# A rebuilt S5 front: injections ahead of one response round, each bank of sums opened once, and 3 of 32 modulation pieces behind the mixer

## The reference, cut to what matters

```python
mod = silu(c) @ w_mod + b_mod                    # 9 rows x 16384 numbers in all
h = modulate(rmsnorm(x, g), sh1, sc1)
lam_bar = exp(lam * dt); b_bar = ((lam_bar - 1) / lam) * b_mat
bu = einsum("blgp,gnp->blgn", u, b_bar)          # 64 groups g of 16 channels p, 64 complex states n
h = associative_scan(h[t] = lam_bar * h[t-1] + bu[t])
y = real(einsum("blgn,gpn->blgp", h, c_mat)) + d_skip * u
a, g = split(gelu(y) @ w_glu); out = a * sigmoid(g)
x = x + ga1 * out
x = x + ga2 * peer(modulate(rmsnorm(x, g2), sh2, sc2))   # gathers 128 expert rows for every row
```

## Time and profile before

| | us |
|---|---|
| timed, median of 3 runs | 3435.63 |
| timed, lowest to highest | 3426.26 to 3446.24 |
| profiled execution: span | 3430.0 |
| busy PE / DVE / ACT / POOL | 2541.4 / 2329.2 / 1302.1 / 1277.8 |
| DMA moved | 1284.73 MB, mean 375 GB/s |

### The profile page before, as it was taken

How to read it: one execution, slowest core, us unless ns; L and a number is a source line. 1 busy time by engine, 2 the same in 40 slices (tenths; PEclk the granted TensorE clock), 3 DMA queues, 4 the chain that set the end, 5 groups by cost and what they waited for, 6 DMA issues and landing times.

```text
span 3430.0 us, 62993 instructions
## 1 busy us (share of the span) xinstructions
PE 2541.4 (74%) x25173; PEld 935.2 (27%) x25173; DVE 2329.2 (68%) x5485; ACT 1302.1 (38%) x4056; POOL 1277.8 (37%) x1133
## 2 busy tenths in 40 slices
PE   4878997868668766668878887878587677666665
PEld 3756322323003200112235452224132032001000
DVE  8753885897866776465553458776888867764655
ACT  3441333333333333344433225553443343333333
POOL 0010343444444444433411227563444444443442
PEclk8979998878667766778999898888787787667667
DMA  9966999999999999999955369999999999999997
GB/s 325 348 241 267 398 413 414 415 403 411 426 426 414 413 426 424 410 420 399 395 180 235 118 227 371 355 411 412 394 421 410 426 421 414 423 425 385 424 426 318
DMA packets 178977, 1284.73 MB, mean 375 GB/s; under 512 B 22264, under 2 KB 23264, under 8 KB 30744
## 3 DMA queue, kind: packets, MB, share of 16 engines
q0 software_dynamic: 151696, 1109.99, 79.0%
q1 hardware_dynamic: 26416, 170.18, 13.1%
q10 hardware_dynamic: 576, 0.59, 0.0%
HBM read 1268.49 MB, written 12.18 MB: 373 GB/s over the span
## 4 chain that ended last, share of the span: by engine, by line
PE 36%; DMA 34%; DVE 19%; ACT 6%; issue 3%; POOL 1%; SPq 0%; another core or an unknown queue 0%; DVEq 0%; ACTq 0%; PEldq 0%; POOLq 0%
DMA arena<-peer_uv,arena 31%; PE psum L2948 13%; DVE arena L2315 9%; PE psum L2875 6%; PE psum L2834 3%; PE psum L3355 2%; DMA arena<-b_mod 2%; PE psum L3106 1%; PE psum L3037 1%; DVE arena L2225 1%; ACT arena L1604 1%; ACT arena L1601 1%; DVE arena L2329 1%; PE psum L2702 1%; DVE arena L1891 1%
## 5 line engine op out<-in xcount | busy, mean ns | idle before, releaser
L2948 PE MATMUL psum<-arena 32*32 32x512 f32 x16384 | 1470.3, 791 | 720.7 <-ACT arena L1604 652.3
L1267 POOL DMA_INDIRECT arena<-peer_uv,arena x1040 | 1160.5, 1116 | 1703.0 <-PE psum L2948 1482.7
L2315 DVE SCALAR_TENSOR_TENSOR arena<-arena 128x1024 f32<-128x1024 f32 x1040 | 1273.5, 1228 | 687.8 <-DMA arena<-peer_uv,arena 670.3
L1591 ACT ACTIVATE arena<-arena 128x1 f32<-128x1 f32 x944 | 190.9, 202 | 1390.8 <-DVE arena L2315 1383.4
L2948 PEld LDWEIGHTS psum<-arena 32*32 32x32 f32 x16384 | 215.8, 117 | 1799.3 <-ACT arena L1604 1584.5
L1604 ACT ACTIVATE arena<-arena 128x32 f32<-128x32 f32 x928 | 298.2, 321 | 30.3
L1601 ACT ACTIVATE arena<-arena 128x1 f32<-128x1 f32 x944 | 277.8, 294 | 30.7
L2875 PEld LDWEIGHTS psum<-arena 128*128 128x128 f32 x2048 | 241.5, 195 | 68.6 <-issue 66.9
L2875 PE MATMUL psum<-arena 128*128 128x128 f32 x2048 | 258.8, 282 | 1.1 <-ACT arena L1528 1.1
L2834 PE MATMUL psum<-arena 128*128 128x512 f32 x256 | 126.0, 625 | 3.2 <-ACT arena L1488 2.4
L2702 PE MATMUL psum<-arena 128*9 128x128 f32 x2048 | 78.8, 317 | 58.4 <-DMA arena<-b_mod 58.3
(11 more groups left out here) (352 smaller groups left out, 2430.8 us busy)
## 6 DMA issues: line engine op xcount, KB each, us to landing
arena<-w_mod SPq DMA_DIRECT2D x64, 1024.0 KB
arena<-peer_wq SPq DMA_DIRECT2D x16, 2048.0 KB, 11.4
arena<-peer_uv,arena POOLq DMA_INDIRECT x1040
arena<-w_glu SPq DMA_DIRECT2D x5, 2048.0 KB, 7.3
arena<-mod_rows SPq DMA_DIRECT2D x5, 1024.0 KB
arena<-w_o SPq DMA_DIRECT2D x1, 4096.0 KB
arena<-x_after_layer SPq DMA_DIRECT2D x7, 512.0 KB
arena<-mod_rows SPq DMA_DIRECT2D x6, 512.0 KB
```

What stands on the lines that cost most here:

```text
L1267: pool.indirect_dma_start(ring[r], None, a[f"peer_uv{t // 5}"], bass.IndirectOffsetOnAxis(ap=ix, axis=0)).then_inc(landed[r], 16)
L1591: act.activation(col, col, ACT.Gelu_apprx_tanh).then_inc(s_gl, 1)
L2315: dve.scalar_tensor_tensor(out=u, in0=u, scalar=GELU_IN if beside_exps(t, m) else 1.0, in1=h, op0=ALU.mult, op1=ALU.mult, accum_out=at(DOT ...
L2948: ins = pe.matmul(acc_of(t, i, c), diag[rows, r, :], ring[r][rows, D + 512 * c:D + 512 * (c + 1)], start=(m == 0), stop=last, skip_group_c ...
```

## The change

The modulation pieces are loaded up to four ahead (`DEEP`), each at places of its own from a written list; where a place is still in use within those four, the load waits for the products that read it. Pieces 29 and 30 are multiplied after the last "y" round and piece 31 after the first `w_glu` products, so 29 pieces instead of 32 stand ahead of the first "y" round. The loads of the first small parameters come first, the prompt rows behind pieces 0 to 3, and the four reads of modulation rows that the norm needs go from SP's queue to ACT's.

The "u" turns are eight rounds of 8 groups. The "i" rounds no longer alternate with "k" rounds; there is one "k" round for all 64 groups, in four column groups, behind the last "i". Its matmuls open each bank once (`start=(slot == 0)`), and 16 small matmuls with the diagonal `d_eye` add the skip term d, so the skip product and its sum on DVE go. The kernel is placed behind a zero pad of 112 columns, so that the "t" matmuls write full width and one ACT copy of 128x2048 replaces four. The copies of "i" rounds 0, 1 and 3 are made by ACT, those of round 2 by DVE. The states are placed in four segments, the first two by ACT as the scan gets there, the last two by DVE. The gelu reads the "y" sums from PSUM. Loops that a counter ran are written out.

```diff
+MOD_TURNS = (29, 30)
+MOD_NORM = 31
+DEEP = 4
...
+        MOD_PLACES = [(MT[0], MT[1]), (MT[2], MT[3]), (MC[0], MC[1]), (MH[0], MH[1]), (MT[0], MT[1]), (MT[2], MT[3]),
...
+                      (MT[0], MT[1]), (MT[2], MT[3]), (MH[0], MH[1]), (MX[0], MX[1]), (MX[2], MX[0]), (MH[0], MH[1]),
+                      (MX[1], MX[2]), (MX[0], MX[1]), (MH[0], MH[1]), (MX[2], MX[0]), (MX[1], MX[2]), (MR[0], MR[1]),
+                      (MJ[0], MJ[1]), (MW[0], MW[1])]
...
-        ROUNDS = ([("m", 0), ("m", 1), ("s", 0)] + [("u", r) for r in range(NR)]
-                  + [("i", 0), ("k", 0), ("m", 2), ("i", 1), ("k", 1), ("m", 3), ("i", 2), ("k", 2), ("i", 3), ("k", 3)]
+        ROUNDS = ([("m", 0), ("m", 1), ("s", 0)] + [("u", r) for r in range(2 * NR)]
+                  + [("i", 0), ("m", 2), ("i", 1), ("m", 3), ("i", 2), ("i", 3), ("k", 0)]
                   + [("t", r) for r in range(NR)] + [("y", r) for r in range(NR)])
-        WHO = {"u": "A", "k": "A", "m": "A", "i": "V", "s": "A", "t": "A", "y": "V"}
-        MOD_AFTER = [("m", 0), ("m", 1), ("s", 0), ("u", 0), ("u", 1), ("u", 2), ("u", 3), ("k", 0),
-                     ("m", 2), ("i", 1), ("k", 1), ("m", 3), ("i", 2), ("k", 2), ("i", 3), ("k", 3)]
...
+        MODS_BEHIND = {("m", 0): (6,), ("m", 1): (7,), ("s", 0): (8,), ("u", 4): (9,), ("u", 7): (10,), ("m", 2): (11,),
+                       ("i", 1): (12,), ("m", 3): (13,), ("i", 2): (14,), ("i", 3): (15, 16), ("k", 0): (17, 18, 19),
+                       ("t", 0): (20,), ("t", 1): (21,), ("t", 2): (22,), ("t", 3): (23, 24, 25, 26, 27, 28),
+                       ("y", 3): MOD_TURNS}
+        BANKS_FREE = {("m", 1): ("m", 0), ("u", 0): ("m", 1), ("u", 1): ("m", 1), **{("u", r): ("u", r - 2) for r in range(2, 8)},
+                      ("i", 0): ("s", 0), ("m", 2): ("u", 7), ("i", 1): ("i", 0), ("m", 3): ("m", 2), ("i", 2): ("i", 1),
+                      ("i", 3): ("m", 3), ("k", 0): ("i", 3), ("t", 0): ("k", 0), ("t", 1): ("t", 0), ("t", 2): ("t", 1),
+                      ("t", 3): ("t", 2), ("y", 0): ("t", 3), ("y", 1): ("i", 2), ("y", 2): ("y", 0), ("y", 3): ("y", 1)}
+        COPIED_BY_VECTOR = [("i", 2)]
...
+            def mod_load(n):
+
+                if n >= DEEP:
+                    sp.wait_ge(s_modmm[n % 2], mods_done(n - DEEP))
+                for k in range(2):
+                    place = MOD_PLACES[n][k]
+                    before = [(m, h) for m in range(n) for h in range(2) if MOD_PLACES[m][h] == place]
+                    if before and before[-1][0] > n - DEEP:
+                        m, h = before[-1]
+                        sp.wait_ge(s_modmm[m % 2], mods_done(m) - 1 + h)
+                    sp.dma_start(at(place, HALF_MOD), a["w_mod"][n][:, k * HALF_MOD:(k + 1) * HALF_MOD]
+                                 ).then_inc(s_modw[n % DEEP], 16)
+                row = 64 * (n % DEEP // 2)
+                sp.dma_start(at(MODB + (n % 2) * MB, MB, row, row + 1), a["b_mod"][n:n + 1, :]
+                             ).then_inc(s_modw[n % DEEP], 16)
+
+            for n in range(MOD_S5):
+                mod_load(n)
...
+            for n in range(MOD_S5, 9):
+                mod_load(n)
+            sp.dma_start(at(DEYE, D, 32, 32 + GP), a["d_eye"]).then_inc(s_dld, 16)
+            sp.dma_start(at(ST0, 2 * HALF * NB), a["state_g"]).then_inc(s_dld, 16)
+            sp.wait_ge(s_blp, 3)
+            mod_load(9)
+            wait_copied(sp, ("s", 0))
+            for n in range(10, 13):
+                mod_load(n)
+            sp.wait_ge(s_mm, round_no[("u", 2 * NR - 1)] + 1)
+            for n in range(13, 21):
+                mod_load(n)
+            sp.wait_ge(s_mm, round_no[("i", NR - 1)] + 1)
+            for n in range(21, MOD_TURNS[0]):
+                mod_load(n)
 
...
+            sp.wait_ge(s_hx, HX_PIECES)
+            for n in MOD_TURNS:
+                mod_load(n)
...
+            mod_load(MOD_NORM)
...
+            pool.wait_ge(s_mm, round_no[("k", 0)] + 1)
+            pool.memset(ksb[:, :, 0:PAD], 0.0).then_inc(s_tz, 1)
...
+            act.dma_start(mod_s, mod_dram[0:1, 0:D].partition_broadcast(P)).then_inc(s_mods5, 16)
+            act.dma_start(mod_a, mod_dram[0:1, D:2 * D].partition_broadcast(P)).then_inc(s_mods5, 16)
+            act.dma_start(at(SHS, D, 0, NB), mod_dram[1:NC9, 0:D]).then_inc(s_mods5, 16)
+            act.dma_start(at(SCS, D, 0, NB), mod_dram[1:NC9, D:2 * D]).then_inc(s_mods5, 16)
...
+                elif kind == "i":
+                    ins = injections(r)
...
-                    out = toep.rearrange("p (r g) m -> p r g m", r=NR)
-                    src = ps.rearrange("p r (g m) -> p r g m", g=4)
-                    for c in range(4):
-                        rows, t0 = slice(32 * c, 32 * c + 32), 32 * c
-                        ins = act.activation(out[rows, :, 4 * r:4 * r + 4, t0:P], src[rows, :, :, t0:P], ACT.Copy)
-                        if c < 3:
-                            link(ins)
+                    ins = act.activation(toep.rearrange("p (r g) m -> p r g m", r=NR)[:, :, 4 * r:4 * r + 4, :],
+                                         ps.rearrange("p r (g m) -> p r g m", g=4), ACT.Copy)
                 elif kind == "s":
...
+            for s in range(2):
+                act.wait_ge(s_scan, SCANNED[s])
+                for gp in range(2):
+                    for k in range(2):
+                        act.activation(hxv[64 * k:64 * k + 64, gp, :, segment(s)],
+                                       hpv[64 * gp:64 * gp + 64, k, :, segment(s)], ACT.Copy).then_inc(s_hx, 1)
+                for m in behind[2 * s:2 * s + 2]:
+                    mod_copy(m)
...
+                act.wait_ge(s_mm, round_no[("y", r)] + 1)
+                ps = half(("y", r)).rearrange("p b (g t q) -> p (b g) t q", g=4, t=TC)
+                for s in range(2):
+                    act.activation(
+                        z5[64 * s:64 * s + 64, :, RG * GP * r:RG * GP * (r + 1)].rearrange("p j (g q) -> p j g q", g=RG),
+                        ps[0:64, :, 4 * s:4 * s + 4, :].rearrange("p g j q -> p j g q"), ACT.Gelu_apprx_tanh
+                    ).then_inc(s_gelu, 1)
+                act.wait_ge(s_gelu, 2 * r + 2)
+                act.activation(at(MS + RG * GP * r, RG * GP, 0, NB).rearrange("p (g q) -> p g q", g=RG),
+                               ps[64:64 + NB, :, 0, :], ACT.Gelu_apprx_tanh).then_inc(s_evA, 1)
...
-                injections(r)
-            wait_copied(dve, ("i", NR - 1))
-            dve.wait_ge(s_mm, round_no[("k", NR - 1)] + 1)
+            injections(2)
+            wait_copied(dve, ("i", 2))
+            wait_copied(dve, ("i", 3))
+            dve.wait_ge(s_modmm[0], mods_done(14))
...
+            dve.wait_ge(s_mm, round_no[("t", NR - 1)] + 1)
+            for s in range(2, NSEG):
+                for gp in range(2):
+                    for k in range(2):
+                        dve.tensor_copy(hxv[64 * k:64 * k + 64, gp, :, segment(s)],
+                                        hpv[64 * gp:64 * gp + 64, k, :, segment(s)]).then_inc(s_hx, 1)
...
-            for r in range(NR):
-                dve.wait_ge(s_mm, round_no[("y", r)] + 1)
-                ps = half(("y", r)).rearrange("p b (g t q) -> p (b g) t q", g=4, t=TC)
-                for s in range(2):
-                    yv = h5[64 * s:64 * s + 64, RG * r:RG * (r + 1)]
-                    tt(yv, yv, ps[0:64, :, 4 * s:4 * s + 4, :], ALU.add)
-                ys = at(MS + RG * GP * r, RG * GP, 0, NB).rearrange("p (g q) -> p g q", g=RG)
-                dve.tensor_tensor(ys, ys, ps[64:64 + NB, :, 0, :], ALU.add).then_inc(s_evV, 1)
...
-                            out = ps[32 * c:32 * c + 32, r, :].rearrange("p (g m) -> p g m", g=4)
-                            ins = pe.matmul(out[:, :, t0:P], at(EYE - GP * odd, 32, 32 * r, 32 * r + GP),
-                                            ksb[r][:, 4 * n_:4 * n_ + 4, 0:P - t0], start=(odd == 0), stop=(odd == 1),
-                                            skip_group_check=True)
+                            ins = pe.matmul(ps[32 * c:32 * c + 32, r, :].rearrange("p (g m) -> p g m", g=4),
+                                            at(EYE - GP * odd, 32, 32 * r, 32 * r + GP),
+                                            ksb[32 * r:32 * r + GP, 4 * n_:4 * n_ + 4, PAD - t0:PAD - t0 + P],
+                                            start=(odd == 0), stop=(odd == 1), skip_group_check=True)
+                ins.then_inc(s_mm, 1)
+
+            def kernels(ps):
+
+                for gl in range(RG):
+                    bank, slot = divmod(gl, 4)
+                    for r in range(NR):
+                        g = RG * r + gl
+                        pe.matmul(ps[32 * r:32 * r + GP, bank, P * slot:P * (slot + 1)], bk[:, g, :],
+                                  cl[:, g, 0:TC, :], start=(slot == 0), stop=False, skip_group_check=True)
+                for bank in range(4):
+                    for r in range(NR):
```

(29 more changed lines are left out.)

509 lines of the change are left out of this document (256 added, 253 removed).

## The result

The changed kernel takes 3396.95 us, median of 6 runs (3385.79 to 3409.22), against 3430.95 us for the kernel before in the same comparison (3418.00 to 3446.24): ratio 0.9903, 95% interval 0.9879 to 0.9927, so 34 us less, between 25 and 42. A second comparison gave 3395.22 and again 0.9903 (0.9883 to 0.9924). Predicted were 3398 and a range of 3376 to 3422.

A forecast was written before the change was run, and what follows sets the result against it. Transfers were taken to pace the kernel after the first gather, and piece loads the front. `w_glu` starting 37.9 us earlier took the profiled 3430.0 to 3392; the median's 5.6 on top gave 3398 us, range 3376 to 3422.

The forecast's parts named there:

- Start, `bl`, compute: Front: piece 0 at 18.5 us, `bl` near 57.3, scan 131 to 176, "k" 4.4 us, states standing at 180.
- The margin: End of the mixer: the states stand at 180 us, 17 us ahead of the loads.
- With loads four deep I take 5.5 us a piece: Front's piece loads: 5.5 us each, between 5.3 and 5.7, instead of 6.29; piece 28 lands at 185 without gaps.
- 8 us, so 193: Loads of pieces 22, 25 and 28: waits for a place, about 2.6 us each, move piece 28's landing from 185 to 193.
- The reads of modulation rows: Front, issued near 49 us: sharing the engines, landed by 57; in order of issue near 77, costing 3 us.
- "y" to `w_glu`: Behind the front: "y" takes 30.8 us from 197, then 10 us in all to `w_glu` at 238.
- My 37.9 us: Start of the `w_glu` products: 238 instead of 275.7 us, the whole predicted saving.
- The start of the sum: Kernel before: profiled execution at 3430.0 us, with the runs' median 5.6 higher.
- Rival 1: Front's loads: 6.29 us a piece is the memory's pace, not the depth's; "y" at 211, 3412 us; chance 0.13.
- Rival 2: Loads moved behind "y" come back as late `w_glu` and query weights, 10 us late, 3416 us; chance 0.07.
- Rival 3: "k": column groups do not overlap or flags order them, +10 us; "y" at 208, 3409 us; chance 0.05.
- Rival 4: Clock stays low from "y" through the first `w_glu` products, +54.6 us, 3453 us; chance 0.05.

The follow-up runs named there:

- the ring: Changed kernel with pieces 22 to 28 taking their halves from a ring of five places; 3395.99 us run once, later median 3396.53, ratio to before 0.9895.
- e1: First run of the ring of five places for the halves of pieces 22 to 28, against the changed kernel; 3395.99 us, timed once.
- The banks: Ring of places plus pieces 16 and 17 taking banks 6 and 7 in turn; 3378.94 us once, later median 3385.86, ratio to before 0.9871.
- e4: Changed kernel with the loops of "k" exchanged, its 64 matmuls issued group by group; 3413.49 us, timed once.
- e2: Changed kernel with loads two deep instead of four; 3426.85 us, timed once.
- e6: Changed kernel with pieces 29 and 30 loaded and multiplied ahead of "y" again; 3404.15 us, median of 5, ratio to before 0.9933.
- e9: The changed kernel again, unedited; median 3395.22 us of 6 runs, ratio to before 0.9903.
- e10: Changed kernel with the ring of five places for pieces 22 to 28, timed again; median 3396.53 us of 6 runs, ratio to before 0.9895.

## Why the prediction was right, and where it was not

- **Start, `bl`, compute.** Piece 0 at 14.75 (18.5 predicted), `bl` at 57.1 (57.3), scan 132.4 to 177.3 (131 to 176), ACT's copies of an "i" round 4.8 us (5.2), "k" 4.3 (4.4). The steps that stand on rows of the same form held. The states were all placed at 198.5, not 180: I had left out that ACT's half (4.36 us, then the sample state) stands behind copies of pieces in its queue. The margin was 12.6 us by the trace, not 17, and only because "y" was late itself.
- **The step that failed: "With loads four deep I take 5.5 us a piece", with the waits for places at "8 us, so 193".** It put the start of piece 28's product at 193; it came at 207, from a start 3.7 us earlier. The pace was right while loads ran (5.3 in the ring). The gaps were mis-sized. By the DMA shares of the three 50 us stretches from 50 to 200 (0.95, 0.77, 0.87), the engines were idle 2.5, 11.5 and 6.5 us, 20.5 in all; that is 12.5 more than I had, of the 17.7 that the step is off, and the rest I can't place. I had counted three waits of 2.6 us for a place, as if the queue behind went on; in the chain each is the rest of a product, an issue and the landing of a half alone. And I had seen that the products of "i", "m" and "k" with their copies delay the pieces between, yet priced nothing for it, because pieces behind were "four deep": near 112 us pieces 12 to 15 lay ready and the load of 16 (issued at 113.49) waited for the products of 12, so the depth was used up while PE did other rounds; and from piece 18 on the places repeat after three pieces or fewer, so they were fewer than the depth. e1 shows the first kind, worth some 7.5 us. The banks show the second: a wait of PE for ACT ahead of piece 16 goes (3.87 us), and "y" comes 4 us earlier. e4 bounds it: of a delay of 9.2 us at 137 some 4 reach "y".
- **The reads of modulation rows.** Issued at 48.05 to 49.3, landed at 62.5 and not at 57; DVE waited 5.41 us for them. With two pieces deep (e2) they were there by 58.3, 8 us after their issue:

```profile
58.27 1.21 DVE L2083 SCALAR_TENSOR_TENSOR arena<-arena 8x1024 f32<-8x1024 f32 x1 [0.47 <-DMA arena<-mod_rows]
```

  The prediction had up to five pieces queued ahead of them. In the changed kernel there were two (5 and 6, multiplied at 53.2 and 60.6), with piece 7 issued right behind at 49.81; in e2 there was one. By an estimate from 415 GB/s, the pace of the stretch, the reads would have landed near 55 with an equal share of the bytes and near 61 in the order of issue (behind 4.2 MB that were left at 47.8); 62.5 is later than either. What the queues moved from 52 to 58 us (packets, MB, share of the engines; q1 is SP's, q10 ACT's):

```profile
q1 hardware_dynamic: 223, 1.63, 65.0%
q10 hardware_dynamic: 227, 0.86, 35.5%
```

  The Trainium skill, DMA: Bandwidth & Descriptors, Queues, rings and completion order, has the engines take turns between queues packet by packet; by that I had priced 1.1 MB at some 6 us, and from the last issue it took 13. The packets of this stretch agree with the page, as many on one queue as on the other, and so do those of e1, e6, e9 and e10 (223 to 226 against 225 to 228). But those of the reads held 3.8 KB and those of the pieces 7.3, so the turns gave the reads a third of the bytes, and from 48 to 52 us their queue had moved only 0.05 MB. In e2 it was 73 packets against 81 from 52 to 54 us, and then SP's queue ran nearly dry (17 against 197 from 54 to 56), which is why the reads were there sooner. Equal turns are not equal bytes. It cost no time, as the states stood ready ahead of "y".
- **"y" to `w_glu`.** 28.6 us (30.8): only the first two groups were at half the rate, 0.70 and 0.63 us against 0.38. Ten us from its end to `w_glu` were 10.3. The first `w_glu` products took 27.7 us, not the 29.41 of the earlier trace rows.
- **Why 3398 was hit all the same.** My 37.9 us stand against 25.7 in the trace. The start of the sum was 3435.63, and the same kernel has 3430.95 with three more runs: 4.7 of it, by luck on the right side. The rest is in the interval of the ratio, 25 to 42 us saved: a gain of 27 to 30, which the first gathers of both profiles show, is compatible with it, and 37.9 is no less so. The times alone could not tell the right sum from the wrong one; the trace did.
- **Rivals.** Rival 1 gave "y" at 211, exactly the measured number, by a mechanism that e1 refutes; a number that fits does not show its cause. Rival 2: the last of the first `w_glu` products end at 277.7 with no wait in them, and the gather follows the start of `w_glu` by 55.4 us against 56.4 before, so nothing came back. Rival 3: e4 shows that the groups overlap. Rival 4: before the last products of pieces, waits of 2.7 to 3.6 us were followed by the half rate (3.3 to 3.6 us for a piece), one of 1.55 us (piece 26) by the full rate (1.94 us), so not every burst behind a wait was slow; and the granted clock was at its higher level (1.00, 2.4 GHz) from 215 us to the end of the first `w_glu` products:

```profile
215.00:250.00 35.00, 32.79 (x403) 31.52 (x401) 3.87 (x2) 15.68 (x22) 0.00 (x0) 1.00 0.53 214
250.00:278.00 28.00, 27.99 (x69) 12.40 (x70) 5.73 (x11) 1.37 (x4) 0.00 (x0) 1.00 1.01 421
```

## What to carry to other kernels

A load depth counts only as far as there are places: list for each load the product that frees its place, and price a shared one with the whole round trip (rest of the product, issue, landing), because an in-order issuing queue stops everything behind it. Where transfers are near the bound, read the DMA share in short stretches before a table of pieces per microsecond is believed: a mean share of 0.87 with full bandwidth in between means waits, not memory. Test a number that fits a rival by an edit that the rival's mechanism forbids. And where executions differ as much as the effect, measure from the last point up to which two kernels are the same: by "y" alone the banks had brought nothing in their first profile and the slower "k" all of its 9.2 us, by the stretch behind the last "i" round 4 us each.
